# Gathers of V and U rows issued in turn, one by one, in a fused attention and expert block

## The reference

```python
h   = RMSNorm(x)
[q|k|v|xc|B|C] = h @ W_in
sb  = StickBreaking(QKNorm(q), QKNorm(k), v)   # 8 heads x 64, strictly causal
cv  = B * causal_depthwise_conv3(C * xc)       # 512 channels
x   = x + concat(RMSNorm(sb), RMSNorm(cv)) @ W_out
h2  = RMSNorm(x)
# PEER: for each token and each of 8 heads, the best 16 of 16384 experts by product keys
u, vv = expert_u[idx], expert_v[idx]           # 128 rows of 1024 of each table, per token
act = gelu(einsum('thkd,td->thk', u, h2))
x   = x + einsum('thk,thkd->td', gate * act, vv)
```

## Time and profile before

| | us |
|---|---|
| median of 3 runs (3340.35 to 3344.33) | 3342.39 |
| profiled execution, its own time | 3333.03 |
| its span | 3331.3 |
| PE busy | 2264.6 |
| DVE busy | 2070.3 |
| POOL busy | 2242.9 |
| ACT busy | 300.9 |
| U gathers (line 390), 1024, busy | 1106.1 |
| V gathers (line 402), 1024, busy | 1133.1 |
| dot products (line 953), 1024, busy | 1233.0 |
| mix (line 592), busy | 1161.1 |
| DMA, mean over the span | 363 GB/s |

### The profile page before, as it was taken

The page is one execution under the profiler, slowest core; times in us unless marked ns, Lnnn a source line. Parts: engine busy times, 40 slices in busy tenths (PEclk is TensorE's granted clock), DMA queues, the critical chain, the costliest instruction groups (busy, mean ns, idle before and its releaser), DMA issues.

```text
span 3331.3 us, 27409 instructions
## 1 busy us (share of the span) xinstructions
PE 2264.6 (68%) x9216; PEld 992.8 (30%) x9216; DVE 2070.3 (62%) x5057; ACT 300.9 (9%) x479; POOL 2242.9 (67%) x2062
## 2 busy tenths in 40 slices
PE   7537856877866578777865668866786665555556
PEld 5424322443322224323321122533442221110011
DVE  3674586555787855565677785545467787444441
ACT  1000100111000001111000000112200000000000
POOL 0245666666776776778777777656667777777775
PEclk9768877976978789688977879966588887788878
DMA  5669999998999999999999999988799999999998
GB/s 192 223 229 409 374 395 342 409 376 287 404 383 385 394 386 409 373 359 333 404 378 387 391 394 390 409 298 315 252 365 376 388 387 373 403 409 410 409 409 324
DMA packets 332349, 1210.54 MB, mean 363 GB/s; under 512 B 37040, under 2 KB 37168, under 8 KB 332208
## 3 DMA queue, kind: packets, MB, share of 16 engines
q0 software_dynamic: 294912, 1073.87, 84.1%
q1 hardware_dynamic: 37296, 134.91, 10.5%
HBM read 1204.44 MB, written 4.19 MB: 363 GB/s over the span
## 4 chain that ended last, share of the span: by engine, by line
POOL 35%; PE 18%; DVE 17%; DMA 14%; issue 13%; ACT 2%; SPq 0%; POOLq 0%; DVEq 0%; ACTq 0%
POOL v_ring L402 18%; POOL u_ring L390 17%; DMA u_ring<-table_u,idx_u 8%; DMA v_ring<-table_v,idx_v 6%; PE acc L592 5%; DVE u_ring L953 5%; PE po L545 3%; PE pt L428 3%; PE pz L525 2%; DVE rc L760 2%; PE pt L417 2%; PE po L428 2%; DVE rb L763 1%; PE pz L422 1%; PE pz L527 1%
## 5 line engine op out<-in xcount | busy, mean ns | idle before, releaser
L953 DVE CUSTOM_DVE_ANT_0 u_ring<-u_ring,h2s 128x1024 f32<-128x1024 f32 x1024 | 1233.0, 1224 | 770.6 <-DMA u_ring<-table_u,idx_u 758.6
L390 POOL DMA_INDIRECT u_ring<-table_u,idx_u x1024 | 1106.1, 1080 | 673.3 <-issue 291.7
L592 PE MATMUL acc<-v_ring,wmask 128*32 128x512 f32 x4096 | 1161.1, 780 | 584.0 <-DMA v_ring<-table_v,idx_v 495.1
L402 POOL DMA_INDIRECT v_ring<-table_v,idx_v x1024 | 1133.1, 1107 | 402.7 <-issue 299.2
L592 PEld LDWEIGHTS acc<-v_ring,wmask 128*32 128x32 f32 x4096 | 204.7, 129 | 1395.8 <-DMA v_ring<-table_v,idx_v 1055.9
L428 PE MATMUL pt<-hT,w_ring 128*128 128x256 f32 (+1 forms) x1440 | 279.2, 351 | 1.1 <-DVE uT L866 1.1
L428 PEld LDWEIGHTS pt<-hT,w_ring 128*128 128x128 f32 x1440 | 238.4, 199 | 47.9 <-issue 24.6
L760 DVE TENSOR_TENSOR_SCAN rc<-rc 128x128 f32<-128x128 f32 (+7 forms) x64 | 84.6, 1349 | 207.8 <-ACT rc L672 207.7
L417 PE MATMUL pt<-ident,rb 128*128 128x128 f32 x416 | 84.6, 365 | 178.5 <-DVE rb L763 130.4
L428 PE MATMUL po<-hT,w_ring 128*128 128x256 f32 (+1 forms) x800 | 155.0, 348 | 7.2 <-ACT kT L650 6.1
L428 PEld LDWEIGHTS po<-hT,w_ring 128*128 128x128 f32 x800 | 130.4, 197 | 39.0 <-issue 26.9
(11 more groups left out here) (131 smaller groups left out, 1681.0 us busy)
## 6 DMA issues: line engine op xcount, KB each, us to landing
w_ring<-wstream SPq DMA_DIRECT2D x240, 512.0 KB, 6.9
u_ring<-table_u,idx_u POOLq DMA_INDIRECT x1024, 7.9
v_ring<-table_v,idx_v POOLq DMA_INDIRECT x1024, 8.0
xs<-x_in_dram SPq DMA_DIRECT2D x8, 512.0 KB, 11.5
y_out_dram<-xs SPq DMA_DIRECT2D x8, 512.0 KB, 6.6
g_all<-norm SPq DMA_DIRECT2D x1, 512.0 KB, 7.5
keysT<-keys SPq DMA_DIRECT2D x1, 128.0 KB, 6.8
chan_sb<-chan SPq DMA_DIRECT2D x1, 19.0 KB, 7.1
```

What stands on the lines that cost most here:

```text
L390: nc.gpsimd.indirect_dma_start(out=u_ring[:, k % U_SLOTS, :], out_offset=None, in_=peer_u, in_offset=bass.IndirectOffsetOnAxis(ap=idx_u[:, ...
L402: nc.gpsimd.indirect_dma_start(out=v_ring[:, slot, :], out_offset=None, in_=peer_v, in_offset=bass.IndirectOffsetOnAxis(ap=idx_v[:, b % ST ...
L592: mm = nc.tensor.matmul(acc[32 * i:32 * i + 32, half * 512:(half + 1) * 512], wmask[:, quarter % 2, i, 32 * j:32 * j + 32], v_ring[:, t % ...
L953: d = V.tensor_tensor_reduce(u, u, h2s[:, b % STASH, :], 1.0, 0.0, ALU.mult, ALU.add, dots[:, quarter % 2, at:at + 1])
```

## The change

POOL's program is rewritten; nothing else is touched. The two waits of a group of U and of a group of V become functions of their own (`u_may`, `v_may`), and `gather_u` and `gather_v` issue one gather each. The loop over s now runs over the four members i of a group: V gather i, then U gather i. The wait of the V group stands before its first gather, as it did; the wait of the U group stands before the first U gather, which now comes after the first V gather in place of after the fourth. Slots, indices and semaphores of each gather are the same. In the first 9 rounds there are only U gathers, in the last 9 only V gathers, in both kernels.

```diff
--- before.py
+++ after.py
@@ -379,36 +379,44 @@
                                     pattern=[[32, 4]], channel_multiplier=-1).then_inc(lane_set, 1)
             nc.gpsimd.memset(wmask[:], 0.0).then_inc(wmask_set, 1)
 
-            def gather_u(s):
+            def u_may(s):
                 b, q = s // GROUPS, s % GROUPS // QGROUPS
                 if s % QGROUPS == 0:
                     pool.wait_ge(idx_ready, picked(b, q))
                 wait(pool, dots_done, s + 1 - U_SLOTS // GROUP)
-                for j in range(GROUP):
-                    k = s * GROUP + j
-                    c = k % PICKS
-                    nc.gpsimd.indirect_dma_start(
-                        out=u_ring[:, k % U_SLOTS, :], out_offset=None, in_=peer_u,
-                        in_offset=bass.IndirectOffsetOnAxis(ap=idx_u[:, b % STASH, c:c + 1], axis=0),
-                    ).then_inc(u_in[k % U_SLOTS], 16)
-
-            def gather_v(g):
+
+            def v_may(g):
                 b, q, j = g // GROUPS, g % GROUPS // QGROUPS, g % QGROUPS
                 if j == 0:
                     pool.wait_ge(idx_kept, picked(b, q))
                 wait(pool, group_done, g + 1 - V_SLOTS // GROUP)
+
+            def gather_u(s, j):
+                k = s * GROUP + j
+                b, c = k // PICKS, k % PICKS
+                nc.gpsimd.indirect_dma_start(
+                    out=u_ring[:, k % U_SLOTS, :], out_offset=None, in_=peer_u,
+                    in_offset=bass.IndirectOffsetOnAxis(ap=idx_u[:, b % STASH, c:c + 1], axis=0),
+                ).then_inc(u_in[k % U_SLOTS], 16)
+
+            def gather_v(g, i):
+                b, q, j = g // GROUPS, g % GROUPS // QGROUPS, g % QGROUPS
+                slot, c = (g * GROUP + i) % V_SLOTS, q * QPICKS + i * QGROUPS + j
+                nc.gpsimd.indirect_dma_start(
+                    out=v_ring[:, slot, :], out_offset=None, in_=peer_v,
+                    in_offset=bass.IndirectOffsetOnAxis(ap=idx_v[:, b % STASH, c:c + 1], axis=0),
+                ).then_inc(v_in[slot], 16)
+
+            for s in range(BLOCKS * GROUPS + V_LAG):
                 for i in range(GROUP):
-                    slot, c = (g * GROUP + i) % V_SLOTS, q * QPICKS + i * QGROUPS + j
-                    nc.gpsimd.indirect_dma_start(
-                        out=v_ring[:, slot, :], out_offset=None, in_=peer_v,
-                        in_offset=bass.IndirectOffsetOnAxis(ap=idx_v[:, b % STASH, c:c + 1], axis=0),
-                    ).then_inc(v_in[slot], 16)
-
-            for s in range(BLOCKS * GROUPS + V_LAG):
-                if s >= V_LAG:
-                    gather_v(s - V_LAG)
-                if s < BLOCKS * GROUPS:
-                    gather_u(s)
+                    if s >= V_LAG:
+                        if i == 0:
+                            v_may(s - V_LAG)
+                        gather_v(s - V_LAG, i)
+                    if s < BLOCKS * GROUPS:
+                        if i == 0:
+                            u_may(s)
+                        gather_u(s, i)
 
         @block.tensor
         def _(pe):
```

## The result

| | before | after |
|---|---|---|
| median of the runs, us | 3342.35 | 3571.47 |
| profiled execution's span, us | 3331.3 | 3575.3 |
| DMA over the span, GB/s | 363 | 339 |
| gathers, busy us (1106.1 + 1133.1; 1124.8 + 1114.7) | 2239.2 | 2239.5 |

The changed kernel is slower by 6.95%: ratio 1.0695, interval 1.0671 to 1.0719. Forecast were 3384 us and a range up to 3450. The sign was right, the size too small by more than five times (229 us for 42).

The account below looks back on a forecast made before the run. It took POOL's gathers (2540 us at best) and DMA transfers (2619 us at 410 GB/s) as both close to the bound. Terms 42 + 0 + 0 + 0 = 42 us gave 3384 us, +1.2%; range 3300 to 3450.

Parts of the forecast that it names:

- The wait for dots moves forward: POOL's wait at U gathers comes 3.7 us earlier: bounds 0 and 126 us, a third taken, +42 us.
- The cover: Queued DMA transfers, some 4 us at a typical moment, hide POOL's later issue except in runs of late groups.
- The three stretches: 913 to 1245, 1660 to 2075, 2490 to 2822 us: ranking and look-up between DVE's dots; 126 us more POOL waits.
- outer bound of 259 us: Extra loss, 385 - 126, if cover failed in 249 to 333 and 2158 to 2407 us; taken as 0.
- The wait for the mix: POOL's wait before a V group, for a group landing at most 3.8 us later: 0, upper bound 163 us.
- Rival C: Much slower: single dots meet gathers at random and late groups come in runs; +113 us, 3456 us, chance 0.14.
- DVE against POOL: Gathers lengthened by dots, in POOL-bound and DVE-rich stretches: bounds -77 and +101 us, 0 taken.
- Rival A: Faster: spread landings let front work fit between dots, so gathers are held less; 3304 us, chance 0.22.
- Rival B: No change: the queue covers the 126 us, passes and ceiling hold the rest; 3342 us within 7, chance 0.14.
- U lands singly: U rows land 2.56 us apart, giving front work room; up to 3.8 us back per group, within the +42 us.
- The last stretch and the stick passes: The last 420 us, at DMA's ceiling, and the 16.8 us passes in 2158 to 2407 us stay unchanged.
- The signs: Dots' wait well above 264 us and 63 times, most new waits 1 to 4 us; ranking stretches' GB/s falls some 10.

Follow-up runs that it names:

- e1: Kernel before, gathers still grouped, only the U group's wait for dots moved to after the first V gather: 3620.48 us, 1.031 of before; again 3621.64, 1.030.
- e3: Changed kernel with V gathers running three gathers further ahead, U and V still alternating: 0.9942, 0.9946 and 0.9968 of before.
- e4: Changed kernel with PE's mix at the last tick of its round in place of the first: 3415.55 us, 0.971 of before; again 3435.58, 0.980.
- e6: Changed kernel with PE's mix at the last tick and dots counted one by one: 3399.06 us, 0.968 of before; in another set 3303.25, 0.989.
- b6: Kernel before (grouped gathers) with PE's mix at the last tick and dots counted one by one: 3315.57 us, 0.992 of before.

## Why the prediction was wrong, step by step

- *The wait for dots moves forward, a third of 126 us.* This is the step that failed, in three places.
  - *The cover.* Two thirds of the 126 us were to be hidden by the queue. The three stretches lost 130 us, so it hid nothing. The 9.1 us of landing time on which the cover rested were the largest of the three; U rows landed in 6.8 us (913 to 1245) and 8.0 us (2490 to 2822) in the median, and after the change in 6.4 (1777 to 2227, before 9.1). Transfers in flight cover a single late group, not a rate that is lower for good.
  - *The rest of the kernel at nothing.* It lost 114 us. Of the outer bound of 259 us, which stood for 249 to 333 and 2158 to 2407 us, these two stretches lost 9 and 5.
  - *The mechanism.* I laid the new stopping time beside the old times of the dots, as if these would not move. That forecast 47 short waits in the three stretches. Measured are 25 there (16 before), but of 6.2 us in the mean (2.4 before) and up to 12.0: 156 us for 39. That the loss there came out at the 126 us of the reading is luck: the reading moves the wait by the same 3.7 us in e1, e3 and the changed kernel, and they lost 3%, nothing and 7%. The loop above decides which, and e3 shows that the same early wait costs nothing when no V row is behind it. (Read again, the rows give 113 to 122 us and 345 to 362 for the 126 and 385 us of the prediction, according to how a group that already waited is counted.)
- *The wait for the mix: 0.* For POOL right: 108.3 us after 103.4. But the step asked only who waits for the mix's end, not what PE holds back while it stands in it. PE's wait for V rows grew from 495.1 to 744.3 us, and behind it stood transposes, key scores and the turn of the picks. That was the missing term; the sum has nothing for it. It cannot be added to the wait for dots, since both are parts of one loop; with it cut, by e3 or e4, the whole loss goes.
- *Rival C* came nearest in size (3456 us). Half of its mechanism, dots that meet the gathers at random, did not come: the gathers' time is 2239.5 us after 2239.2, so the middle value of 0 for DVE against POOL was right. *Rival A* needed shorter gathers and didn't come. *Rival B*, no change, needed the cover of the queue and didn't come either.
- *U lands singly*, as a gain, is not shown: 12 us between e6 and b6 are all that the runs have for it, and e3 fits as well with the early wait costing nothing by itself.
- *The last stretch and the stick passes* stay, as forecast (first to last scan of line 760 from 2167.6 us on, 230.3 us before and 231.2 after). The signs were half right: the waits rose far above 264 us, but of the 34 groups that waited anew 20 waited for longer than 4 us, and DMA's rate fell by 22 to 56 GB/s and not by some 10. Three dots from the end of the changed kernel's quiet stretch, 2.56 us apart, with 1.33 us of idle before each:

```profile
3300.72 1.23 DVE L961 CUSTOM_DVE_ANT_0 u_ring<-u_ring,h2s 128x1024 f32<-128x1024 f32 x1 [1.33 <-DMA u_ring<-table_u,idx_u]
...
3303.28 1.23 DVE L961 CUSTOM_DVE_ANT_0 u_ring<-u_ring,h2s 128x1024 f32<-128x1024 f32 x1 [1.33 <-DMA u_ring<-table_u,idx_u]
...
3305.84 1.23 DVE L961 CUSTOM_DVE_ANT_0 u_ring<-u_ring,h2s 128x1024 f32<-128x1024 f32 x1 [1.32 <-DMA u_ring<-table_u,idx_u]
```

## What to carry to other kernels

When a wait moves up in an in-order queue, list what stands behind it and follow each item until it either ends or comes back to what the wait is for. If it comes back, the delay can be paid in every round, and a sum made with the old times of the releaser cannot tell which order pays it: here it gave the same for kernels that lost nothing and 7%. The cuts that worked here are to issue first what other engines stand for, to place an engine's blocking wait after the short steps that others need, and to release slots one by one.

## What the runs showed of the hardware

- A gather by POOL, 0.94 us alone, that meets a dot on DVE ends 0.81 us after that dot's end; in the trace before this is so, at 0.8 to 0.9 us, for 341 of the 381 gathers that began during a dot and met no second one. It does not hold the other way: 701 dots there began while a gather was under way, and took 1.223 us in the mean, as all do. The sum of the gathers' surplus was 0.31 us a dot in both kernels; in other kernels here, and on the slower chips, POOL is busy for up to 70 us more.
- The same kernel took 3339 to 3342 us in some sets and 3508 to 3516 in others. In the last slices, with no front work on any engine, the changed kernel's trace of the latter kind shows 364 to 368 GB/s where the former shows 409 to 410. It is not a lower ceiling throughout: e4's first run, on a chip of the slower kind, moved 409 GB/s from 250 to 340 and from 1280 to 1365 us. Slices of the changed kernel's run in such a set:

```profile
GB/s 198 204 294 366 356 273 339 389 317 326 294 356 349 326 381 369 317 331 333 313 339 317 324 304 374 361 254 309 269 347 327 304 306 298 349 364 364 365 368 315
```

The ratio of the changed kernel hardly moved (1.066 and 1.070), while e6's did (0.968 and 0.989). Why these chips move less in the last stretch is open.
